# Inverting the 8x8 diagonal blocks by substitution on the vector engine in a hybrid DeltaNet / PEER layer

## The reference

```python
lmat = jnp.where(strict, jnp.einsum('nbhid,nbhjd->nbhij', kb, kc) * decay, 0.0)
amat = lmat + jnp.eye(DN_CHUNK, dtype=lmat.dtype)
sol = lax.linalg.triangular_solve(amat, rhs, left_side=True, lower=True, unit_diagonal=True)
...
v_new = u_i - jnp.einsum('bhck,bhkv->bhcv', w_i, s)
s_next = s * jnp.exp(gl_i)[..., None, None] + jnp.einsum('bhck,bhcv->bhkv', kd_i, v_new)
```

## Time and profile before

| | |
|---|---|
| median of three runs | 2081.66 us (2079.07 to 2082.28) |
| the profiled execution | 2085.01 us |
| its span | 2082.7 us |
| mean granted clock of TensorE | 0.989 of full speed |
| TensorE busy, share of the span | 97% |
| DVE busy, share of the span | 72% |

### The profile page before, as it was taken

One profiled execution on the slowest core, in us unless ns is written; L12 is line 12 of the kernel. 1 busy time (PEld: TensorE's weight loads), 2 busy tenths in 40 slices (PEclk: granted clock), 3 DMA queues, 4 the chain that ended last, 5 costly groups with the idle time before them and its releaser, 6 DMA issues.

```text
span 2082.7 us, 39418 instructions
## 1 busy us (share of the span) xinstructions
PE 2018.6 (97%) x13846; PEld 1796.5 (86%) x13846; DVE 1495.8 (72%) x3294; ACT 969.0 (47%) x1743; POOL 1027.0 (49%) x641
## 2 busy tenths in 40 slices
PE   5899999999999998999999999999999999999997
PEld 2688888888887887889999999999998888888886
DVE  4777777777641117779889867777548888888888
ACT  3545545455443234333343378888633333333332
POOL 0345544435534457445899866666763322222222
PEclk8899999999999999999999999999999999999999
DMA  6323232223213345334788879999999999999993
GB/s 266 116 77 108 87 97 72 97 84 100 82 51 111 121 143 182 114 112 133 218 292 274 276 256 356 363 361 360 386 367 360 383 376 347 369 341 356 355 353 121
DMA packets 151780, 470.04 MB, mean 226 GB/s; under 512 B 15632, under 2 KB 46576, under 8 KB 148464
## 3 DMA queue, kind: packets, MB, share of 16 engines
q1 hardware_dynamic: 108064, 300.13, 42.3%
q0 software_dynamic: 36864, 134.23, 17.6%
q10 hardware_dynamic: 6736, 34.08, 4.1%
HBM read 415.38 MB, written 53.00 MB: 225 GB/s over the span
## 4 chain that ended last, share of the span: by engine, by line
PE 89%; DVE 4%; POOL 3%; DMA 1%; ACT 1%; issue 1%; SPq 1%; POOLq 0%; ACTq 0%; DVEq 0%
PE bank L2925 25%; PE bank L591 14%; PE bank L593 14%; PE bank L592 14%; PE bank L2912 4%; POOL w_lo L1287 2%; PE pair L591 2%; PE bank L2514 1%; PE bank L2524 1%; PE pair L592 1%; PE pair L593 1%; PE bank L2487 1%; PE pair L2487 1%; PE pair L2586 1%; PE pair L2564 1%
## 5 line engine op out<-in xcount | busy, mean ns | idle before, releaser
L591 PE MATMUL bank<-lat_hi,w_hi 128*128 128x384 f32 (+2 forms) x1488 | 536.3, 360 | 4.4 <-DVE lat_lo L2022 2.6
L1287 POOL TENSOR_TENSOR w_lo<-raw,w_hi 128x1024 fp32r<-128x1024 f32 x148 | 361.7, 2445 | 346.8 <-ACT w_hi L1024 163.2
L593 PE MATMUL bank<-lat_hi,w_lo 128*128 128x384 f32 (+2 forms) x1488 | 521.7, 351 | 0.0
L592 PE MATMUL bank<-lat_lo,w_hi 128*128 128x384 f32 (+2 forms) x1488 | 521.3, 350 | 0.0
L1426 POOL DMA_INDIRECT rows<-peer_v,e_row x128 | 136.4, 1066 | 337.8 <-DVE pair L2240 317.8
L591 PEld LDWEIGHTS bank<-lat_hi,w_hi 128*128 128x128 f32 x1488 | 281.6, 189 | 18.9 <-issue 4.5
L593 PEld LDWEIGHTS bank<-lat_hi,w_lo 128*128 128x128 f32 x1488 | 280.7, 189 | 17.7
L592 PEld LDWEIGHTS bank<-lat_lo,w_hi 128*128 128x128 f32 x1488 | 281.5, 189 | 13.4 <-issue 0.2
L1287 POOL TENSOR_TENSOR w_lo<-raw_more,w_hi 128x1024 fp32r<-128x1024 f32 x80 | 196.7, 2462 | 94.7 <-ACT w_hi L1024 65.6
L2925 PE MATMUL bank<-w_hi,c_lo 128*128 128x512 f32 x768 | 237.1, 389 | 0.0
L2925 PE MATMUL bank<-w_hi,c_hi 128*128 128x512 f32 x768 | 237.1, 389 | 0.0
(11 more groups left out here) (398 smaller groups left out, 3699.4 us busy)
## 6 DMA issues: line engine op xcount, KB each, us to landing
raw<-w SPq DMA_DIRECT2D x210, 512.0 KB
raw_more<-w SPq DMA_DIRECT2D x142, 512.0 KB
g_dram<-gs ACTq DMA_DIRECT2D x24, 1024.0 KB
gu_dram<-gu SPq DMA_DIRECT2D x120, 192.0 KB
gq<-g_dram SPq DMA_DIRECT2D x45, 512.0 KB
gl<-gu_dram SPq DMA_DIRECT2D x28, 768.0 KB
ada<-w_ada SPq DMA_DIRECT2D x32, 512.0 KB, 3.6
dY<-gc_dram SPq DMA_DIRECT2D x8, 768.0 KB, 4.2
```

The lines of the kernel that those rows point to most:

```text
L591: nc.tensor.matmul(out, hi, rh, start=start, stop=False)
L592: nc.tensor.matmul(out, hi, rl, start=False, stop=False)
L593: return nc.tensor.matmul(out, lo, rh, start=False, stop=stop)
L1287: nc.gpsimd.tensor_sub(w_lo[:, slot, :], raw_at(slot % 2 if src is None else src), w_hi[:, slot, :].bitcast(F32)).then_inc(split_done, 1)
```

## The change

The 8x8 diagonal blocks are inverted by substitution on DVE, and levels 0, 1 and 2 on TensorE go away (FIRST = 3). `pack_blocks` masks `Lt` into `T`, sums its 64 columns to 8 per chunk, mirrors rows for the other direction by a shuffle of partitions, and leaves strictly triangular 8x8 blocks of all 12 units in `sub_x` (96 columns). `substitute` does steps j = 1 to 6, each a shuffle that spreads row j of each block, a product, and a sum over the first j columns, each waiting for the one ahead. `unpack_blocks` mirrors back, adds the diagonal, spreads into `XTh`, and transposes 32x32 squares into `Xh`. The scratch is in PSUM bank 6.

Moved as well: on DVE `scale_output`, the decays, `decay_sums`, `key_norms`, `couple` and `modulation` stand at other steps of the scan; the two first taps of Q_LAT stand ahead of the levels; heads 1 to 6 are written out in place of the loop. On TensorE K_LAT blocks 0 to 2 stand ahead of the levels, followed by the turning of the context chunks (`context_by_token`, which waits for `XTh`) and the sums of squares; `key_products` goes from slot (3, 2) to (3, 1) and `sum_columns` from (3, 0) to (3, 2), into bank 1. On ACT the identities go away and `weigh_part` 0 and 1 stand at level 5 and behind `diagonal_xt`. On POOL `normalise` goes ahead of `lo(3)`.

The diff, cut to its core (left out: declarations, the constants, renumbered semaphore counts, the same moves for head 0):

```diff
 
-                for lv in range(1, LEVELS - 1):
+                next_hi(h, 3)
+                for lv in range(FIRST, LEVELS - 1):
                     for g in range(2):
-                        act.wait_ge(xt_done, h * 18 + (2 * (lv - 1) + g + 1))
+                        act.wait_ge(xt_done, h * 14 + (2 * (lv - FIRST) + g + 1))
+                        if lv == FIRST:
+                            act.wait_ge(xt_done, h * 14 + 2)
                         nc.scalar.copy(as_pairs(flat3(W[:, 3 * g:3 * g + 3, :]), lv),
                                        pairs(XTh, lv, 3 * g, 3)).then_inc(w_done, 1)
-                    if lv == 1:
-                        next_hi(h, 3)
-                    if lv == 3:
-                        weigh_part(h, 0)
-                    if lv == 5:
-                        weigh_part(h, 1)
-                    if lv == 2:
+                    if lv == FIRST:
                         act.wait_ge(qts_done, h * 2)
                         act.wait_ge(kk, h * 3)
                         silu_of(h, Q_LAT)
                         square_q(h)
-                    if lv == 4:
+                    if lv == FIRST + 1:
                         act.wait_ge(qts_ld, h * 16 + 16)
                         q_row = qTs[:, :, :, :].rearrange("p a b c -> p (a b c)")
                         nc.scalar.activation(q_row, q_row, ACT.Exp).then_inc(qts_exp, 1)
+                    if lv == FIRST + 2:
+                        weigh_part(h, 0)
                 diagonal_xt(h)
+                weigh_part(h, 1)
...
-                exp_decay(n, range(0, 4))
-                identity_x(n)
-                exp_decay(n, range(4, 8))
-                identity_xt(n)
+                exp_decay(n, range(0, 8))
...
-                lo(3, h * 4 + 8)
                 if fin:
                     normalise(h - 1)
+                lo(3, h * 4 + 8)
...
+            def place(offset, j):
+
+                return bank[6][:, offset:offset + NU * j]
+
+            packed, step_row, step_part, final = (place(i * NU * BLK, BLK) for i in range(4))
+
+            def by_unit(ap):
+
+                return ap.rearrange("p (d c j) -> p d c j", d=NDIR, c=NCH)
+
+            def found_columns(j):
+
+                return bass.AP(sub_x[:, :, :, :].tensor, 0,
+                               [[NU * BLK, P], [NCH * BLK + BLK - j, NDIR], [BLK, NCH], [1, j]])
+
+            def factor_column(j):
+
+                return bass.AP(sub_x[:, :, :, :].tensor, j,
+                               [[NU * BLK, P], [NCH * BLK + BLK - 1 - 2 * j, NDIR], [BLK, NCH], [0, j]])
+
+            in_block = [i // BLK * BLK for i in range(32)]
+            turned_block = [b + BLK - 1 - i % BLK for i, b in enumerate(in_block)]
+
+            def pack_blocks(n):
 
                 dve.wait_ge(lt, (n + 1) * (NG + NCH))
                 for z in range(2):
-                    nc.vector.tensor_tensor(W[half(z), 3 * g:3 * g + 3, :], Lt[half(z), 3 * g:3 * g + 3, half(z)],
-                                            rep(cst[half(z), C_LVL:C_LVL + HB], 3), ALU.mult).then_inc(mask_t, 1)
-
-            def first_transposed(n, g):
-
-                dve.wait_ge(id_done, n * 2 + 3)
-                dve.wait_ge(mask_t, n * 4 + 2 * (g + 1))
-                xt_v = pairs(XTh, 0, 3 * g, 3)
-                nc.vector.tensor_tensor(xt_v, xt_v, as_pairs(flat3(W[:, 3 * g:3 * g + 3, :]), 0), ALU.add).then_inc(xt_done, 1)
-
-            def first_plain(n, g):
-
-                dve.wait_ge(mx_mm, n * 14 + (g + 1))
-                dve.wait_ge(id_done, n * 2 + 2)
-                x_v = pairs(Xh, 0, 3 * g, 3)
-                nc.vector.tensor_tensor(x_v, x_v, as_pairs(bank[3 + g][:, 0:3 * HB], 0), ALU.add).then_inc(x_done, 1)
+                    nc.vector.tensor_tensor(T[half(z), :, :], Lt[half(z), :, half(z)],
+                                            rep(cst[half(z), C_NEAR:C_NEAR + HB], NCH), ALU.mult).then_inc(sub_done, 1)
+                dve.wait_ge(sub_done, n * N_SUB + 2)
+                nc.vector.tensor_reduce(packed[:, 0:NCH * BLK].rearrange("p (c r) -> p c r", r=BLK),
+                                        T[:, :, :].rearrange("p c (q r) -> p c r q", r=BLK), AX.X, ALU.add
+                                        ).then_inc(sub_done, 1)
+                dve.wait_ge(sub_done, n * N_SUB + 3)
+                nc.vector.stream_shuffle(packed[:, NCH * BLK:], packed[:, 0:NCH * BLK], turned_block).then_inc(sub_done, 1)
+                dve.wait_ge(sub_done, n * N_SUB + 4)
+                for d in range(NDIR):
+                    strict = rep(cst[:, C_STRICT + d * BLK:C_STRICT + (d + 1) * BLK], NCH)
+                    last = nc.vector.tensor_tensor(sub_x[:, d, :, :], by_unit(packed)[:, d], strict, ALU.mult)
+                last.then_inc(sub_done, 1)
+
+            def substitute(n, steps):
+
+                for j in steps:
+                    done = n * N_SUB + 5 + 3 * (j - 1)
+                    row, part = (by_unit(t[:, 0:NU * j]) for t in (step_row, step_part))
+                    dve.wait_ge(sub_done, done)
+                    nc.vector.stream_shuffle(row, found_columns(j), [b + j for b in in_block]).then_inc(sub_done, 1)
+                    dve.wait_ge(sub_done, done + 1)
+                    nc.vector.tensor_tensor(part, row, factor_column(j), ALU.mult).then_inc(sub_done, 1)
+                    dve.wait_ge(sub_done, done + 2)
+                    nc.vector.tensor_tensor(found_columns(j), found_columns(j), part, ALU.add).then_inc(sub_done, 1)
+
+            def unpack_blocks(n):
+
+                done = n * N_SUB + N_SUB - 3
+                dve.wait_ge(sub_done, done)
+                nc.vector.tensor_copy(final[:, 0:NCH * BLK].rearrange("p (c r) -> p c r", r=BLK),
+                                      sub_x[:, 0, :, :]).then_inc(sub_done, 1)
+                nc.vector.stream_shuffle(final[:, NCH * BLK:], flat3(sub_x[:, 1, :, :]), turned_block).then_inc(sub_done, 1)
+                dve.wait_ge(sub_done, done + 2)
+                whole = packed.rearrange("p (u r) -> p u r", r=BLK)
+                nc.vector.tensor_tensor(whole, final.rearrange("p (u r) -> p u r", r=BLK),
+                                        rep(cst[:, C_DIAG:C_DIAG + BLK], NU), ALU.add).then_inc(sub_done, 1)
+                dve.wait_ge(sub_done, done + 3)
+                dve.wait_ge(id_done, 1)
+                own = cst[:, C_BLK:C_BLK + HB // BLK].unsqueeze(1).unsqueeze(3).to_broadcast([P, NCH, HB // BLK, BLK])
+                for d in range(NDIR):
+                    nc.vector.tensor_tensor(XTh[:, d, :, :].rearrange("p c (q r) -> p c q r", r=BLK),
+                                            whole[:, d * NCH:(d + 1) * NCH, :].unsqueeze(2).to_broadcast(
+                                                [P, NCH, HB // BLK, BLK]), own, ALU.mult).then_inc(xt_done, 1)
+                for d in range(NDIR):
+                    dve.wait_ge(xt_done, n * 14 + d + 1)
+                    nc.vector.transpose(flat3(Xh[:, 1 - d, :, :]), flat3(XTh[:, d, :, :])).then_inc(x_done, 1)
...
                 tap = conv_of(h, Q_LAT)
                 if fin:
                     gate_output(h - 1)
-                for lv in range(1, LEVELS):
+                tap(0)
+                tap(1)
+                for lv in range(FIRST, LEVELS):
+                    i = lv - FIRST
...
-                    if lv == 1:
-                        tap(0)
-                    if lv == 2:
+                    if lv == FIRST:
                         tap(2)
                         tap(3)
                         if fin:
                             output_norms(h - 1, bank[4][:, 3 * P:3 * P + LAT])
-                    if lv == 4:
+                    if lv == FIRST + 2:
                         attention(h, 2)
...
-                    if lv == 1:
-                        tap(1)
-                    if lv == 3:
+                    if lv == FIRST + 1:
                         attention(h, 0)
                         attention(h, 1)
-                    if lv == 4:
+                    if lv == FIRST + 2:
                         attention(h, 3)
 
...
@@ -1802,16 +1852,17 @@
                     if more:
                         if s == 0:
                             middle_weights(n)
-                            decay(n, range(0, 4))
                         if s == 1:
-                            decay(n, range(8, NU))
+                            if fin:
+                                scale_output(h - 1)
+                            decay(n, range(4, 8))
                         if s in (2, 3):
                             tap(0)
                         if s == 4:
-                            key_norms(n)
+                            for c in (2, 3, 4, 5, 0, 1):
+                                couple(n, c)
                         if s == 5:
-                            for c in range(CT):
-                                couple(n, c)
+                            substitute(n, range(1, 3))
```

(101 more changed lines are left out.)

43 lines of the change are left out of this document (15 added, 28 removed).

## The result

The changed kernel takes 2099.9 us (four runs, 2099.9 to 2100.8), the kernel before, on the same chip, 2080.4 (2078.7 to 2082.3). The ratio is 1.0091, with a 95% interval of 1.0078 to 1.0104: slower by 0.9%, where 2066 was predicted. Times are medians of all runs of a kernel; ratios leave out three slow ones (2510.6 us with the decays back, 11452 and 9095 us of the kernel before). The first solve of the scan of head 0 starts at 122.1 us instead of 123.3; head 7's starts at 573.6 instead of 554.8. So all that was lost was lost in the seven heads between, 19.9 us. Behind head 7 the profiled execution is even 3.4 us shorter than the one before, but there the clock fell three times in the profile of before and cost 5 us of TensorE's work, and never in this one.

A forecast was written before the change was run, and what follows sets the result against it. TensorE's stream was taken to bound the heads. Gains of 32.7 us less losses of 16.6 (sums 9.1, clock 4.5, small 3) net 16.1: profiled 2085.0 becomes 2068.9, median 2066; range 2045 to 2084.

The forecast's parts named there:

- TensorE loses 46 us of work: Levels 0 to 2 leave TensorE's stream: some 5.8 us a head, 46 us for eight heads, the most the change can bring.
- The chain's price: Dependent DVE steps cost 0.19 us plus 1 us per 960 columns; substitution steps 3 to 6 take 3.1 us, unpacking 2.8.
- Rival D: DVE's chain steps cost 0.4 us, not 0.2: 24 us more than the likeliest case, 2090 us, slower; chance 0.15.
- The K_LAT blocks wait for `gate_output`: Heads 1 to 6: TensorE stands 2.2 us, bounds 1.2 and 3.2, because `gate_output` comes behind the whole unpacking on DVE.
- Head 0 gains 2.6: In head 0 DVE's 10 us chain runs bare, from 94 to 104; gain 2.6 us (0 to 5).
- Head 7 gains 4.6, with waits of 1.2: Head 7 has no K_LAT blocks; waits 0.4 us for `XTh`, then for the squares, in all 1.2; gains 4.6.
- `scale_output` gains 0.65 a head: Leaving the gap before step 1's residual saves 0.65 of the 0.8 us wait in six heads: 3.9 us.
- The sums lose 9.1 us, between 2.5 and 17.5: `decay_sums` at the end of step 2: one POOL collision plus lateness, 1.3 us in each of seven scans (bounds 0.35, 2.5).
- The 0.35 us by which the sums were to be late: Step 3's residual comes 0.35 us late even undisturbed, as DVE's last taps end 0.5 us after step 3 has begun.
- The clock costs 4.5 us, 0 to 9: A 2.2 us stall may drop the clock in a head, costing 1.5 us; half of six heads taken, 4.5 us.

The follow-up runs named there:

- the other repairs: Changed kernel, POOL's additions waiting, plus `gate_output` before transpositions, context chunks first, head 0's POOL lo(1), lo(2) after packing, `middle_weights` on ACT: 2040.6 us, 0.9802.
- the run with POOL's wait: Changed kernel, sums still at the end of step 2, POOL's two additions of part 3 and lo(0) waiting until the sums are done: 2052.5 us, 0.9859.

## Why the prediction was wrong

What the change does by itself, on TensorE and on DVE, was forecast rightly; the sum was wrong by the place of one moved helper and the clock behind it. Step by step:

- *TensorE loses 46 us of work*: right. It is busy for 30.6 less, although the lower clock took more of its busy time over the whole program, 28.4 us of lost work against 14.9: together 44.
- *The chain's price* (0.19 us plus 1 us per 960 columns): right. Steps 3 to 6 took 3.0 us (3.1 foreseen), the unpacking 2.6 (2.8), a 48-column shuffle 0.21. Rival D has nothing left.
- *The K_LAT blocks wait for `gate_output`*, 2.2 us in six heads: 1.9. Taking 7.0 of the 11.4 us away, and 1.4 in head 7, gave 9.
- *Head 0 gains 2.6*: 1.2. Its bare chain was 1.7 us longer by the lock on the packing, which I had not looked for there.
- *Head 7 gains 4.6, with waits of 1.2*: TensorE waits 0.33 us for `XTh` as foreseen, but then 1.99 for POOL's `sqo_t`, and the clock falls behind that (1.6 us of lost work). From the starts of the last two scans, less the stall and what the clock lost behind it, I estimate a gain of some 3.
- *`scale_output` gains 0.65 a head*: the wait is 0.3 instead of 0.8, so 0.5.
- *The sums lose 9.1 us, between 2.5 and 17.5*: this is the step that failed. "I take one" collision, at 0.95 us, was three, at 1.1, 1.1 and 2.1. They cost 6 x 4.43 + 4.26 = 31 us of stall. The 0.35 us by which the sums were to be late even undisturbed is 0.1 here, and no wait at all shows where POOL keeps away. I had the time of POOL's additions right (5.5 us into step 2; "5.8") and the lock, and even said that a sum which starts with POOL's addition waits for all of it. But I took one collision out of two that I had seen, and left out the third partner: `lo(0)`, which before ran 2.6 us behind the additions, clear of all, now stands directly behind them, since it is the additions that the moved decays made 3.4 us later in the step (from 2.1 to 5.5), and `lo(0)` only 0.9. By the Trainium skill ("SBUF — State Buffer", SBUF: two separate sides) a DVE operation with two inputs in SBUF and a GpSimd operation that reads SBUF exclude each other for a whole instruction; the trace agrees, 2.56 us beside a `lo(0)` of 2.52. I laid this on one of POOL's instructions there, and not on each.
- *The clock costs 4.5 us, 0 to 9*: 18; the second step that failed. I tied it to the wait for `gate_output`. That one, 1.9 us, left the clock at 1.00 in all six heads of the changed kernel; it was the 4.4 us stall, which I did not foresee, behind which it was at 0.50 in each of seven scans.

So 13.6 us of forecast loss (9.1 and 4.5) were 49; 2066 with these 35 more is 2101, and 2099.9 was measured; that it comes so near is in part luck, for the smaller terms above miss by 1 to 2 us each, both ways. The rival on the slow side, D, was looked for in the chain's price, the part that was new, and not in the moved steps, where the price of a collision was known from a row (1.24 against 0.28) and only their number was guessed.

What is shown: that the collision is the loss (moving the sums gave 41 us, making POOL wait 47, and putting the decays back 34), that either of two moves taken back removes it, and that its size goes with the number of POOL's instructions met. The clock's share is shown to be a price of its own: two scans have a stall of 2.1 and 2.3 us and no fall. Not shown is when the clock falls. It fell behind all seven stalls of 4.3 to 4.4 us, but the runs without them still have falls elsewhere, with 1.6 to 8.4 us of lost work where the changed kernel has 18.3.

## What to carry to other kernels

When a step with two SBUF operands is moved on DVE, lay POOL's whole queue over its new place, not the one instruction that is seen there, and count one collision for each DVE instruction that may meet one of POOL's; moving a producer of POOL's work moves POOL too. A short step that is on nobody's path becomes the path if it stands ahead of one that is, and a stall of TensorE is paid again in clock. Before giving up a change that lost, take back the small moves one by one: here a wait of POOL turned 0.9% lost into 1.4% gained, and the other repairs made it 2%.

## What the runs showed of the hardware

- Whether POOL holds up DVE went with the operands of DVE's instruction. The sums (two inputs in SBUF) took 1.5 to 2.56 us instead of 0.42; a copy of three columns from SBUF to SBUF took 0.79 us on average instead of 0.17 (0.92 at 508.65, where POOL's addition ran to 509.54); but two transpositions of 384 columns from SBUF to SBUF, beside POOL's `lo` from 487.80 to 490.16, took 1.03 us at 488.59 and as much in all other heads (mean 550 ns each), and the spreads, one input in PSUM, 1.02.
- The granted clock after a stall is not a matter of its length alone: behind 1.9 us it stayed at full in all six heads of the changed kernel but fell once in the run with POOL's wait (at 161 us, behind the wait that ended at 160.0) and once with the decays back (at 281 us), behind 2.2 us it fell in two of six heads of the run with the sums in step 3, behind 2.0 us in head 7 of the changed kernel it fell (at 558 us), behind 2.1 to 2.3 us it fell in five of seven scans, behind the stall of 4.3 to 4.4 us in all seven. In the changed kernel a fall lasted some 3 us at 141 and at 558 us (1.6 us of lost work each), and 6 to 7 us behind the six stalls of 4.4 us (2.3 to 2.6 each).
- A 12-column shuffle lasts 0.18 us, one of 72 columns 0.23, its pattern load 0.01 to 0.02: no dearer than a product of the same size.
